# A mixture-of-experts layer on one core: 64-row tiles computed in two parts, down pieces split later

## The reference, cut to what matters

```
h = x + W_out [ attention(head group A) || mLSTM(head group B) ]      # of RMSNorm(x)
out = h + hier_moe(RMSNorm(h))

def hier_moe(t):          # 1024 rows of 1024, 16 experts in 4 groups, hidden width 512
    grp   = best of 4 groups (softmax);   top 2 of the 4 experts in it
    for e in range(16):
        hid = silu(t @ w_gate[e]) * (t @ w_up[e])
        y  += combine[:, e] * (hid @ w_down[e])
```

## Time and profile before

| | |
|---|---|
| median of 3 runs | 978.54 us (977.75 to 980.79) |
| the profiled execution's own time | 978.41 us |
| its span, first to last instruction | 976.6 us |
| granted TensorE clock, mean | 0.96 of full speed |
| PE busy | 871.4 us, 89% of the span |
| VectorE busy | 613.8 us, 63% |
| ScalarE busy | 541.3 us, 55% |
| GpSimd busy | 247.2 us, 25% |

### The profile page before, as it was taken

The page is one execution under the profiler, slowest core; times in us unless marked ns, Lnnn a source line. Parts: engine busy times, 40 slices in busy tenths (PEclk is TensorE's granted clock), DMA queues, the critical chain, the costliest instruction groups (busy, mean ns, idle before and its releaser), DMA issues.

```text
span 976.6 us, 17186 instructions
## 1 busy us (share of the span) xinstructions
PE 871.4 (89%) x4977; PEld 684.7 (70%) x4978; DVE 613.8 (63%) x1252; ACT 541.3 (55%) x970; POOL 247.2 (25%) x371
## 2 busy tenths in 40 slices
PE   3889999999999977699984699999999999999993
PEld 2769888898988856488873556664658588666883
DVE  1766666666666657244467857556459589955991
ACT  2463746546375555112124358656559589865981
POOL 3101011010101100000004134244244454634452
PEclk9999999999999996899995799999999999999997
DMA  8720100101000050344465686694789899979973
GB/s 254 253 69 11 35 22 21 43 0 43 21 21 22 1 194 22 128 153 163 139 213 180 256 272 227 235 311 108 279 290 318 290 333 380 345 244 326 331 278 65
DMA packets 57646, 168.41 MB, mean 172 GB/s; under 512 B 12584, under 2 KB 14928, under 8 KB 57616
## 3 DMA queue, kind: packets, MB, share of 16 engines
q1 hardware_dynamic: 50384, 143.13, 40.8%
q0 software_dynamic: 7232, 24.92, 9.8%
HBM read 143.49 MB, written 24.54 MB: 172 GB/s over the span
## 4 chain that ended last, share of the span: by engine, by line
PE 81%; ACT 5%; issue 5%; DVE 4%; DMA 3%; POOL 1%; ACTq 0%; SPq 0%; POOLq 0%; DVEq 0%
PE bank_j L967 14%; PE bank_j L969 13%; PE bank_j L968 13%; PE bank_j L1063 6%; PE bank_j L1308 5%; PE bank_s L1329 3%; PE bank_t L961 3%; PE bank_j L1074 3%; PE bank_o L1054 3%; ACT w_high L672 2%; PE bank_t L1047 2%; PE bank_j L1313 2%; DMA hn<-ffn_in,row_g 1%; PE bank_s L1039 1%; PE bank_t L1096 1%
## 5 line engine op out<-in xcount | busy, mean ns | idle before, releaser
L967 PE MATMUL bank_j<-w_high,rows_high 128*128 128x512 f32 x512 | 206.5, 403 | 11.0 <-DVE w_low L1526 8.7
L968 PE MATMUL bank_j<-w_low,rows_high 128*128 128x512 f32 x512 | 201.1, 393 | 0.0
L969 PE MATMUL bank_j<-w_high,rows_low 128*128 128x512 f32 x512 | 201.0, 393 | 0.0
L573 POOL TENSOR_TENSOR tick<-mhalf 1x1 f32<-1x1 f32 x152 | 87.9, 583 | 219.7 <-ACT lg L874 73.7
L967 PEld LDWEIGHTS bank_j<-w_high,rows_high 128*128 128x128 f32 x512 | 97.0, 189 | 42.7 <-issue 19.3
L1770 DVE TENSOR_TENSOR w_low<-w_res,w_high 128x1024 fp32r<-128x1024 f32 x96 | 114.1, 1217 | 5.6 <-issue 3.7
L969 PEld LDWEIGHTS bank_j<-w_high,rows_low 128*128 128x128 f32 x512 | 97.0, 189 | 21.0
L968 PEld LDWEIGHTS bank_j<-w_low,rows_high 128*128 128x128 f32 x512 | 97.1, 190 | 18.4
L672 ACT ACTIVATE w_high<-w_res 128x1024 fp32r<-128x1024 f32 x96 | 97.9, 1055 | 2.5 <-PE bank_j L969 2.4
L961 PE MATMUL bank_t<-ident,hn 128*128 128x128 f32 x336 | 46.8, 285 | 17.3 <-DMA hn<-mix_rows 7.5
L1063 PE MATMUL bank_j<-hnT,w_res 128*128 128x128 f32 x512 | 60.3, 276 | 0.0
(11 more groups left out here) (382 smaller groups left out, 1801.9 us busy)
## 6 DMA issues: line engine op xcount, KB each, us to landing
w_res<-in_w_gate_dram SPq DMA_DIRECT2D x48, 512.0 KB, 3.6
w_res<-in_w_up_dram SPq DMA_DIRECT2D x48, 512.0 KB
bias<-in_w_down_dram SPq DMA_DIRECT2D x32, 512.0 KB
slot_b<-in_w_gate_dram SPq DMA_DIRECT2D x16, 512.0 KB
PT<-in_w_up_dram SPq DMA_DIRECT2D x16, 512.0 KB
gmix<-in_w_down_dram SPq DMA_DIRECT2D x16, 512.0 KB
h<-in_w_down_dram SPq DMA_DIRECT2D x16, 512.0 KB
hn<-in_x_dram SPq DMA_DIRECT2D x8, 512.0 KB, 3.4
```

The lines of the kernel that those rows point to most:

```text
L573: pool.tensor_tensor(tick[:, len(ticks):len(ticks) + 1], mhalf[0:1, 0:1], mhalf[0:1, 0:1], ALU.mult)
L967: pe.matmul(out_, ah, bh, start=start, stop=False)
L968: pe.matmul(out_, ah, bl, start=False, stop=False)
L969: return pe.matmul(out_, al, bh, start=False, stop=stop)
```

## The change

It has three parts.
1. `half_tile` works in two parts. Part 0 computes columns 0 to 127 of both sides, gate and up, over all 8 row chunks into J0; part 1 the other 128 columns into J1. Each part has its own silu, its own multiply, its own transpose and its own copy. The transpose of part 0 stands ahead of `rows_T`, that of part 1 behind the first down piece; the down pieces go in the order 0, 2, 1, 3. SyncE's waits move with this: gate and up pieces are free in part 1.
2. The down pieces of expert e are split at the head of full tile e (behind the half tiles of e), no longer at the tail of full tile e-1.
3. In a full tile on ScalarE, `rows_raw` stands behind piece 5, no longer behind piece 7.

```diff
+        half_order = [0, 2, 1, 3]
...
                     if i < 2 * FC:
-                        sp.wait_ge(pe_gup, full * (FC + 1) + i // 2 + 1)
+                        sp.wait_ge(pe_gup, full * (FC + 1) + i // 2 + 2)
                     else:
-                        sp.wait_ge(pe_dnp, full * FC + i - 2 * FC + 1)
+                        sp.wait_ge(pe_dnp, full * FC + half_order.index(i - 2 * FC) + 1)
...
-            def tile(t, split):
-
+            def tile(t, e, split):                                    # ScalarE
+
+                for i in range(2 * FC, PIECES):
+                    split_hi(e, i, t - 1)
                 act.activation(warm[:, 0:1], warm[:, 1:2], ACT.Silu)
...
-                split(5, 2 * FC)
+                split(5, 6)
                 rows_raw(t + 1)
+                split(6, 2 * FC)
                 weigh(t)
-                split(2 * FC, PIECES)
...
-                act.wait_ge(pe_gup, (FC + 1) * (t + 2))                # half_tile, ScalarE
-                wait(act, dve_mh, 2 * t)
-                act.activation(sg[:, 0:HF], J0[:, 0:HF], ACT.Silu).then_inc(act_silu, 2)
-                act.wait_ge(pe_hT, 2 * t + 2)
-                wait(act, pe_dnp, FC * (t + 1))
-                cp(raw_hidden.rearrange("p a b -> p (a b)"), S0[:, 0:HF])\
-                    .then_inc(act_hT, 2)
+                for part in range(2):
+                    act.wait_ge(pe_gup, (FC + 1) * (t + 1) + (1 if part == 0 else FC + 1))
+                    wait(act, dve_mh, 2 * t)
+                    act.activation(sg[:, part * P:(part + 1) * P], (J0, J1)[part][:, 0:P], ACT.Silu).then_inc(act_silu, 1)
+                for part in range(2):
+                    act.wait_ge(pe_hT, 2 * t + part + 1)
+                    wait(act, pe_dnp, FC * (t + 1))
+                    cp(raw_hidden[:, part, :], (S0, X0)[part][:, 0:P]).then_inc(act_hT, 1)
...
+            def half_hidden_T(t, part):                               # TensorE
+                pe.wait_ge(dve_mh, 2 * t + part + 1)
+                if part == 0:
+                    wait(pe, dve_hT, 2 * t)
+                pe.transpose((S0, X0)[part][:, 0:P], mh[:, part * P:(part + 1) * P], ident[:, :]).then_inc(pe_hT, 1)
...
+                for part, bank in enumerate((J0, J1)):
+                    for k in range(KC):
+                        j, kk = k // 2, k % 2
...
+                        cols = [slice(side * HF + part * P, side * HF + (part + 1) * P) for side in range(2)]
+                        for g in range(1 if j < 3 else 2):
                             for side in range(2):
+                                out_ = bank[side * HP:(side + 1) * HP, 0:2 * P] if j < 3 else \
+                                    bank[side * HP:(side + 1) * HP, g * P:(g + 1) * P]
+                                b = raw_both[j][:, :, kk, cols[side]] if j < 3 else raw_gu[j][g][:, kk, cols[side]]
+                                ins = pe.matmul(out_, raw_rows[:, k, :], b, start=(k == 0), stop=(k == KC - 1),
+                                                skip_group_check=True)
+                        if part == 1 and kk == 1:
+                            ins.then_inc(pe_gup, 1)
+                    if part == 0:
+                        ins.then_inc(pe_gup, 1)
+                half_hidden_T(t, 0)
                 rows_T(t + 1)
...
-                pe.wait_ge(act_hT, 2 * t + 2)
-                for c in range(FC):
+                for n, c in enumerate(half_order):
+                    if n == 1:
+                        half_hidden_T(t, 1)
+                    if n % 2 == 0:
+                        pe.wait_ge(act_hT, 2 * t + n // 2 + 1)
...
+                for part in range(2):                                 # half_tile, VectorE
+                    dve.wait_ge(act_silu, 2 * t + part + 1)
+                    wait(dve, pe_hT, 2 * t)
+                    at = slice(part * P, (part + 1) * P)
+                    dve.tensor_tensor(mh[:, at], sg[:, at], (J0, J1)[part][:, P:2 * P], ALU.mult).then_inc(dve_mh, 1)
...
-            def tile(t, split):
+            def tile(t, e, split):                                    # VectorE
+                for i in range(2 * FC, PIECES):
+                    split_lo(e, i)
                 wait(dve, act_y, t)
...
                 weigh(t)
-                split(2 * FC, PIECES)
```

More of the change, by code:

```diff
@@ L899, in _ @@
             route_exp(TILES - EARLY, 2)
-            for i in range(2 * FC, PIECES):
-                split_hi(0, i, None)
             act.wait_ge(dve_tab, 1)
@@ L951, in split @@
                         split_hi(e + 1, i, last)
-                tile(last, split)
-            tile(inner_tiles(NE - 1), lambda a, b: None)
+                tile(last, e, split)
+            tile(inner_tiles(NE - 1), NE - 1, lambda a, b: None)
         @block.tensor
@@ L1298, in half_tile @@
                 wait(pe, dve_mh, 2 * t)
[L1300 to L1311, removed]
-                            for side in range(2):
[L1313 to L1317, removed]
@@ new lines, in half_tile @@
+                for part, bank in enumerate((J0, J1)):
+                    for k in range(KC):
+                        j, kk = k // 2, k % 2
+                        if part == 0 and kk == 0:
+                            for i in (k, k + 1):
+                                pe.wait_ge(ld_piece[i], e * 16 + (48 if i < OUTP else 32))
+                        cols = [slice(side * HF + part * P, side * HF + (part + 1) * P) for side in range(2)]
+                        for g in range(1 if j < 3 else 2):
+                            for side in range(2):
+                                out_ = bank[side * HP:(side + 1) * HP, 0:2 * P] if j < 3 else \
[7 more added lines that the diff above has]
+                        ins.then_inc(pe_gup, 1)
@@ L1329, in half_tile @@
                         ins = pe.matmul(S1[side * HP:(side + 1) * HP, :], raw_hidden[:, c % 2, c // 2 * HP:(c // 2 + 1) * HP],
-                                        slot[2 * FC + c][:, side * HALF:(side + 1) * HALF], start=(c == 0), stop=(c == FC - 1))
+                                        slot[2 * FC + c][:, side * HALF:(side + 1) * HALF], start=(n == 0), stop=(n == FC - 1))
                     ins.then_inc(pe_dnp, 1)
@@ L1892, in half_tile @@
                 pick_weights(t)
-                dve.wait_ge(act_silu, 2 * t + 2)
-                wait(dve, pe_hT, 2 * t)
-                dve.tensor_tensor(mh[:, 0:HF], sg[:, 0:HF], J0[:, HF:], ALU.mult).then_inc(dve_mh, 2)
+                for part in range(2):
[3 more added lines that the diff above has]
+                    dve.tensor_tensor(mh[:, at], sg[:, at], (J0, J1)[part][:, P:2 * P], ALU.mult).then_inc(dve_mh, 1)
                 dve.wait_ge(act_hT, 2 * t + 2)
@@ L1936, in _ @@
             columns()
-            for i in range(2 * FC, PIECES):
-                split_lo(0, i)
             dve.wait_ge(dve_tab, 1)
```

## The result

The changed kernel takes 1008.1 us (median, 1005.0 to 1009.9) against 979.2 (977.8 to 980.8) for the kernel before: ratio 1.029, 95% interval 1.026 to 1.032. It is slower by 29 us. The forecast was 974.1, with a range of 963 to 981.

The account below looks back on a forecast made before the run. The prediction took TensorE, busy 89% of the span, as the bound, with gains only from gaps between its instructions. Seven passages gain 2.5, the adjacent pair 2.3, less 0.5: 4.3 us off 978.41, so 974.1, range 963 to 981.

Parts of the forecast that it names:

- the adjacent pair: Two half tiles in succession (the eighth passage): 24.8 us against 27.1, a gain of 2.3.
- L: Landing of the full tile's scatter, which `weigh_half` waits for, counted from that tile's end: 16.55 us against 19.05 before.
- a passage of 31.8: Half tile plus following full tile, seven times: L + 15.25 = 31.8 us against 32.16, a gain of 0.35 each.
- the rival with L = 17.5: Landing counts from the start of the scatter's issue, so a shorter issue gains nothing: 980.8 us, chance 0.20.
- L + 7.0: When TensorE's transposes of hidden rows can start in the full tile: 7.0 us behind the scatter's landing.
- full tiles in a row: VectorE enters the following full tile 0.25 us late in three places: 0.5 us off the gain.
- 8.24: Time in us TensorE needs from the hidden-row transposes to the end of the full tile.
- a wait of 1.9: New TensorE wait for VectorE's multiply at a full tile's first hidden-row transposes: 1.9 us, seven times.
- the forecast gain of 2.5: Gain over the seven single passages: 0.35 us each, 2.5 us in all.
- The formula: Whole change in us from the landing time L alone: faster below L = 16.75, slower above 17.6.
- The rival on the other side: GpSimd not released earlier, L stays at 19.0, new head bounds at full price: 991.5 us, chance 0.08.
- The rival without a shorter half tile: Narrow products or switches keep the half tile as long; only the adjacent pair's 2.3 lost: 976.4 us, chance 0.10.

Follow-up runs that it names:

- own_result: Changed kernel plus a separate result buffer for half tiles, so weighting a half tile no longer waits for the preceding full tile's scatter: 966.9 us, ratio 0.987.
- head_only: Kernel before with part 2 of the change alone (down splits at the head of their full tile): 993.7 us, ratio 1.016.
- halves_alone: Kernel before with part 1 of the change alone (half tile in two parts): 980.1 us, ratio 1.001.
- warm_first: Changed kernel with ScalarE's one-element silu, which loads the table, moved ahead of the down splits: 1002.0 us, ratio 1.026.
- raw_early: Kernel before with part 3 of the change alone (`rows_raw` behind piece 5): 988.4 us, ratio 1.011.
- halves_tail: Changed kernel with the down splits back at the tail of the full tile before (parts 1 and 3 without part 2): 989.6 us, ratio 1.013.
- own_tail: Kernel before with parts 1 and 3 of the change and a separate result buffer for half tiles: 987.3 us, ratio 1.012.

## Why the prediction was wrong

**The path was right.** The half tile is 12.3 long (forecast 12.0), the wait for `rows_raw` is gone, the scatter starts 1.7 behind `weigh` and issues in 1.6, TensorE waits in a full tile's first transposes for the multiply, in seven passages, and the adjacent pair gains 2.1 (forecast 2.3). Everything hangs on L, as forecast; own_result shows it. The sum on that path was wrong in three terms. Forecast was a passage of 31.8; measured is 35.92 on average over seven.

1. **The landing, +0.7 a passage.** L was taken as 8.45 behind the end of the scatter's issue, 16.55. It is 17.28 on average (16.9 to 17.8), 9.5 behind the end of the issue. From the start of the issue it is 11.1 (577.39 to 588.51; 10.6 to 11.5 in the seven), against 10.9 before the change (574.87 to 585.73). So beside the loads the landing stays nearly fixed to the start: the rival with L = 17.5 was right on this term. An issue that is 0.8 shorter brought the landing at most some 0.3 nearer (10.6 from the start in head_only against 10.9; 11.1 in the changed kernel against 11.3 in halves_alone, whose loads are as late), no more than one passage differs from the next. Seven times 0.7 is 5.1 us.
2. **The table load, +1.3 a passage.** "L + 7.0" to the transposes was read from full tiles in a row, where the splits followed other copies and no load lay between. Measured is L + 8.32 in every passage. The forecast moved the splits to the head of the loop's body and did not ask which table ScalarE has there. 9.2 us. This term is read from the trace, where the load of 1.28 stands in line between `weigh_half` and the first split; no run takes it away from there (warm_first only changes which load it is).
3. **What follows the wait, above all the clock, +2.1 a passage.** From the transposes to the end of the full tile the forecast took 8.24 from the earlier trace rows. Measured is 10.32 on average (9.8 to 11.0), and 8.5 with the wait filled by idle work. The forecast saw a wait of 1.9 and counted only its length. It is 3.5 with the first two terms, and the time behind it runs in part at half speed. The clock is 1.8 of the 2.1, which is what the idle work takes away, 12.5 us in all; the other 0.3 (2 us) stands in head_only as well, where the clock stayed up (8.5 again), and its cause is open. The clock is the largest term, and no rival had it.

Together 0.73 + 1.32 + 2.08 = 4.1 a passage, 28.9 us for the seven; with the forecast gain of 2.5 there, the seven passages lose 26.4 (from the half tile's start to that of the tile behind the full tile they add up to 251.4, where seven times 32.16 is 225.1). The expert part loses 26.1: full tiles in a row lose another 2.4 (forecast 0.5), of which 1.5 goes with the second load in warm_first, the pair gains 2.1, and the first full tile and what follows the last one are 0.7 shorter together. The other 3 us of the 29 lie ahead of the expert part, where they vary from kernel to kernel; no run here ties them to the change.

**The formula** "change = 7 x (L - 16.9) - 1.8" gives 0.9 us for the measured L. So the rival on the landing would have been no better: it gave 980.8. The rival on the other side asked for L = 19.0 and had the loss at 13 us; L never went there. The rival without a shorter half tile did not happen. The range ended at 981, and the worst case of all at 991.5, because every case was built on L alone, with the cost behind L and the speed of TensorE held fixed.

**What was in sight.** In the trace of the kernel before the granted clock is 1.00 through every passage, although TensorE waits three times in each (0.93, 0.37 and 0.69). The change took the first of these waits and made one of 3.5. raw_early shows how near to the edge the kernel before was: the same waits moved together, by one of them, cost 8 us.

How the clock is decided is open. Waits of 1.35 and 0.69 with two transposes between made it fall in five stretches of eight and left it up in three that look the same; single waits of 2.2 did so in four of eight in halves_tail and again in own_tail; waits of 1.2 to 1.5 within full tiles in head_only never did; waits of 3.0 to 3.9 in the changed kernel always did, and the longest of them was followed by 3.4 at half clock, not by 6.8. What is shown is that the fall follows idle time of TensorE, and goes when that time is filled.

## What to carry to other kernels

Before work is put behind a wait that costs nothing today, price the whole chain from that wait to the bounding engine, with the table that ScalarE holds at that place; and if the chain comes out late, see first whether the wait can be taken away (here one more buffer turned +29 us into -18, with one table load moved). A gap of TensorE is to be counted with what follows it: here waits of 2 to 4 us, single or close behind each other, were followed by 3.4 or 6.8 us at half clock, those of 3 and more each time and those of some 2 in about half of the cases. Removing a short wait can lose time when another engine makes the bounding one wait at a later place, where the waits add up.

## What the runs showed of the hardware

- Each stretch at half clock between the end of the first full tile and the start of the last was 3.4 or 6.8 us long, in the five traces that have any. One of 3.4 cost 1.65 us in raw_early.
- Idle transposes that nobody reads took 0.12 us each (24 in 2.78) and kept the clock up.
- A scatter with add of 128 rows of 4 KB beside weight loads landed 11.1 us behind the start of its issue with an issue of 1.6 (the changed kernel), and 10.9 with one of 2.4 (the kernel before). In head_only, with an issue of 1.6 as well, it was 10.6.
- The issue of a scatter lasts longer where a split of VectorE is already running at its start. In the kernel before, timeline of VectorE, for the issue of 2.44 at 574.87:

```profile
574.58 1.22 DVE L1770 TENSOR_TENSOR w_low<-h,w_high 128x1024 fp32r<-128x1024 f32 x1
```

  A split that begins right behind the start leaves it at 1.6. In own_tail, between two full tiles:

```profile
756.08 1.62 POOL L623 DMA_INDIRECT out_dram<-lg,row_s  x1 [0.16 <-issue]
756.19 1.22 DVE L1789 TENSOR_TENSOR w_low<-w_res,w_high 128x1024 fp32r<-128x1024 f32 x1
```

  The fourteen traces have 224 issues of 128 rows: the 106 that began under a split took 2.4, the other 118 took 1.6, and in 27 of these a split began later within the issue. The Trainium skill, "SBUF — State Buffer", section "Who interferes with whom", says that a VectorE instruction with two SBUF inputs contends with a GpSimd instruction that reads SBUF, and infers that it leaves the writing of descriptors alone. The prediction took the 2.4 for a sign against that inference. It is none: only a split that is under way when the issue starts lengthens it.
